# Gated delta rule steps with one combined product per chunk, and five modulation chunks summed later, in a two-block transformer kernel

## The reference, cut to what matters

```python
def step(S, inp):                       # one chunk of 64 tokens, per head
    qd, kc, val, att, kt, cd = inp
    v_new = val - kc @ S
    o = qd @ S + att @ v_new
    S = S * cd + kt.T @ v_new
    return S, o
# kc and val come from a 64x64 unit triangular solve per chunk and head
...
mod = silu(c) @ w_ada + b_ada           # 12 chunks of 512 columns
sh1, sc1, g1, sh2, sc2, g2 = split(mod, 6)
h = rmsnorm(x, norm_mix) * (1 + sc1) + sh1
proj = h @ w_in                         # 16 chunks of 512 columns
...
x = x + g1 * (merged @ w_out)
h2 = rmsnorm(x, norm_ffn) * (1 + sc2) + sh2
x = x + g2 * moe(h2)                    # 32 experts, top 2
```

## Time and profile before

| | |
|---|---|
| median of 3 runs | 1138.16 us (1137.22 to 1146.73) |
| profiled execution, its own time | 1137.32 us |
| its span | 1135.5 us, so 1.8 us lie around it |
| granted TensorE clock, mean | 0.998 |
| TensorE busy (PE) | 1106.6 us, 97% |
| TensorE weight loads (PEld) | 843.2 us, 74% |
| VectorE (DVE) | 603.9 us, 53% |
| ScalarE (ACT) | 501.5 us, 44% |
| GpSimd (POOL) | 151.2 us, 13% |
| delta steps | about 141.5 to 168 us of the span |
| feed-forward part begins | 192.6 us |
| product of step s = 3 ends | 427.1 us |

### The profile page before, as it was taken

The page is one execution under the profiler, slowest core; times in us unless marked ns, Lnnn a source line. Parts: engine busy times, 40 slices in busy tenths (PEclk is TensorE's granted clock), DMA queues, the critical chain, the costliest instruction groups (busy, mean ns, idle before and its releaser), DMA issues.

```text
span 1135.5 us, 18601 instructions
## 1 busy us (share of the span) xinstructions
PE 1106.6 (97%) x7625; PEld 843.2 (74%) x7625; DVE 603.9 (53%) x925; ACT 501.5 (44%) x827; POOL 151.2 (13%) x111
## 2 busy tenths in 40 slices
PE   8999799999999999999999999999999999999996
PEld 7987678999878888778888876666666666666663
DVE  5988676879956784785755652222222222222223
ACT  6665654654433746645556252222222222222223
POOL 1339960422000040400000000000000000000000
PEclk9999999999999999999999999999999999999999
DMA  9862825477486756644548579999999999999994
GB/s 314 280 215 77 297 93 201 161 263 257 183 306 204 243 176 223 211 162 154 174 157 329 209 288 423 421 426 423 423 425 420 425 422 421 425 424 421 426 421 175
DMA packets 82701, 332.05 MB, mean 292 GB/s; under 512 B 4555, under 2 KB 6926, under 8 KB 66110
## 3 DMA queue, kind: packets, MB, share of 16 engines
q1 hardware_dynamic: 81236, 328.43, 74.6%
q0 software_dynamic: 1088, 2.34, 1.0%
q10 hardware_dynamic: 298, 0.11, 0.1%
HBM read 329.83 MB, written 1.05 MB: 291 GB/s over the span
## 4 chain that ended last, share of the span: by engine, by line
PE 80%; DVE 8%; DMA 7%; issue 2%; ACT 2%; SPq 1%; DVEq 0%; ACTq 0%
PE bank L1113 18%; PE bank L451 12%; PE bank L453 12%; PE bank L452 12%; PE bank L1132 9%; PE bank L1103 5%; DMA ring<-in_w_exp_down 3%; DVE ring_r L1844 2%; DMA ring<-in_w_in 2%; DVE arena L1924 2%; PE bank L1160 1%; PE bank L1161 1%; DMA ring<-in_w_ff 1%; DMA ring<-in_w_ada 1%; PE bank L1120 1%
## 5 line engine op out<-in xcount | busy, mean ns | idle before, releaser
L1844 DVE TENSOR_TENSOR ring_r<-ring,arena_r 128x2048 fp32r<-128x2048 f32 x93 | 217.9, 2355 | 118.5 <-ACT arena_r L1333 116.9
L1333 ACT ACTIVATE arena_r<-ring 128x2048 fp32r<-128x2048 f32 x93 | 177.4, 1918 | 170.1 <-PE bank L453 71.7
L453 PE MATMUL bank<-arena_r,actT_r 128*128 128x512 f32 x384 | 150.5, 392 | 0.0
L451 PE MATMUL bank<-arena_r,tok_r 128*128 128x512 f32 x352 | 140.8, 400 | 1.7 <-DVE con L2331 1.7
L452 PE MATMUL bank<-ring_r,tok_r 128*128 128x512 f32 x352 | 138.2, 393 | 0.0
L2688 POOL TENSOR_TENSOR ring<-ring 128x512 f32<-128x512 f32 x63 | 102.5, 1652 | 253.7 <-ACT ring L1424 251.9
L2503 DVE TENSOR_TENSOR arena<-bank,arena 64x512 f32<-64x512 f32 x62 | 42.7, 688 | 175.3 <-PE bank L1132 174.6
L451 PE MATMUL bank<-tok_r,arena_r 128*128 128x256 f32 x352 | 99.5, 283 | 1.8 <-DVE actT_r L1861 1.2
L453 PE MATMUL bank<-tok_r,ring_r 128*128 128x256 f32 x352 | 98.3, 279 | 0.0
L452 PE MATMUL bank<-actT_r,arena_r 128*128 128x256 f32 x352 | 98.2, 279 | 0.0
L2489 DVE TENSOR_TENSOR arena<-bank,arena 128x256 f32<-128x256 f32 x32 | 13.6, 425 | 151.3 <-ACT arena L1763 93.9
(11 more groups left out here) (424 smaller groups left out, 1770.7 us busy)
## 6 DMA issues: line engine op xcount, KB each, us to landing
ring<-in_w_in SPq DMA_DIRECT2D x22, 2048.0 KB, 9.6
ring<-in_w_exp_down SPq DMA_DIRECT2D x22, 2048.0 KB, 21.3
ring<-in_w_exp_gate SPq DMA_DIRECT2D x21, 2048.0 KB, 21.9
arena<-in_w_exp_up SPq DMA_DIRECT2D x21, 2048.0 KB, 23.5
ring<-in_w_ff SPq DMA_DIRECT2D x16, 2048.0 KB, 7.8
ring<-in_w_ada SPq DMA_DIRECT2D x12, 2048.0 KB, 10.9
arena<-in_w_exp_gate SPq DMA_DIRECT2D x11, 2048.0 KB, 21.5
arena<-in_w_exp_down SPq DMA_DIRECT2D x10, 2048.0 KB, 21.4
```

The lines of the kernel that those rows point to most:

```text
L451: mm(o, l[0], r[0], start=start, stop=False)
L453: return mm(o, l[1], r[0], start=False, stop=stop)
L1333: A(hi, w, ACT.Copy).then_inc(S["w_high"], 1)
L1844: TT(half(i, ringR)[0], w, hi.bitcast(fp32), ALU.subtract).then_inc(S["w_rest"], 1)
```

## The change

It does four things.
1. `kc` and `qd` of a chunk stand side by side in `KQ`, so that one product of 128 rows gives both the correction and the output's state part. The masked products of two chunks are made together, behind step 1 and step 3, in two different quadrants of the array, into the banks of the combined products. The two `kc` banks of a t are filled in turns.
2. VectorE multiplies the old state by its decay before the product for the new state is there, and adds afterwards (two instructions in place of four). VectorE's other work in the steps is put in another order: `o_squares(0)`, `att_out(0)` and `w_rest(F0)` come later, and the second attention product is split into two parts.
3. Modulation chunks 0 to 4 leave the mixing stage. Chunk 0 is now summed by VectorE before `add_x`, 1 and 2 take the places of 5 and 6, 3 that of 7, and 7 and 8 move back by one place or more; 6, 4 and 5 are summed by VectorE in `steps2`, s = 3, 9 and 13. GpSimd does not sum anything in the mixing stage any more.
4. The order of the loads follows.

```diff
-        ET, DI, DT, YY, AT, MT = [x[:, 0:8 * C] for x in (ar(15360, 1024), DQ, DK, QD, kbT, qT)]
-        VAL, KC, VN = KB, QD, ar(15360, 1024)
+        ET, DI, DT, RR, AT, MT = [x[:, 0:8 * C] for x in (ar(15360, 1024), DQ, DK, QD, kbT, qT)]
+        YY = DQ[:, 8 * C:16 * C]
+        VAL, VN = KB, ar(15360, 1024)
+        KQ = [QD, qdT]
...
-        ADA_BY_POOL = (0, 4)
-        ADA_BY_DVE = (7, 8, 9)
-        DVE_MOD = {4: 8, 10: 9}
-        ADA_FF1 = {2: 5, 5: 6}
-        ADA_FF2 = {1: 7, 3: 8, 6: 9}
-        ADA_STEP = {3: 10, 6: 11}
+        ADA_BY_POOL = (1, 2, 10, 11)
+        ADA_BY_DVE = (0, 3, 7, 8, 9, 6, 4, 5)
+        DVE_FF2 = {3: 7, 5: 8, 10: 9}
+        DVE_STEP = {3: 6, 9: 4, 13: 5}
+        ADA_FF1 = {2: 1, 5: 2}
+        ADA_FF2 = {1: 3, 3: 7, 4: 8, 6: 9}
+        ADA_STEP = {3: 10, 4: 6, 6: 11, 10: 4, 14: 5}
...
-        ADA_BEHIND = {("win", 2): (0,), ("win", 6): (1, 2, 3, 4), ("ff1", 2): (5,), ("ff1", 5): (6,), ("ff2", 0): (7,),
-                      ("ff2", 3): (8,), ("ff2", 6): (9,), ("win2", 2): (10,), ("win2", 6): (11,)}
+        ADA_BEHIND = {("wout", 1): (0,), ("ff1", 2): (1,), ("ff1", 5): (2,), ("ff2", 0): (3,), ("ff2", 3): (7,),
+                      ("ff2", 4): (8,), ("ff2", 6): (9,), ("win2", 2): (10,), ("win2", 4): (6,), ("win2", 6): (11,),
+                      ("win2", 9): (4,), ("win2", 13): (5,)}
...
-                elif l == 1:
-                    ada(0)
                 elif l == 2:
-                    ada(1)
                     att_turn()
...
                     bk = begin(f"vp{n}")
                     for h in range(DH):
-                        o = (4 * t + h) * P
-                        i = mm(bk[r:r + C, h * P:(h + 1) * P], KC[:, o + r:o + r + C], old[:, h * P:(h + 1) * P],
-                               start=True, stop=True)
+                        i = mm(bk[:, h * P:(h + 1) * P], KQ[t][:, 256 * h + 2 * r:256 * h + 2 * r + P],
+                               old[:, h * P:(h + 1) * P], start=(h == 0), stop=True, skip_group_check=True)
                     end(i, f"vp{n}")
                     if n == 1:
                         prob_turn(range(4, 8))
+                    elif n == 2:
+                        end(att_values(begin("ao0"), 0, range(8)), "ao0")
                     else:
-                        att_values(n - 2)
-                        if n == 3:
-                            o_turn(0)
-                pe.wait_ge(S["vn_new"], n + 1)
+                        end(att_values(ao1, 1, range(4, 8)), "ao1")
+                    wait_read(pe, f"vp{n}")
...
-                bk = begin(f"do{n}")
-                for h in range(DH):
-                    ...
-                    if n:
-                        mm(bk[r:r + C, h * P:(h + 1) * P], qdT[:, o + r:o + r + C], old[:, h * P:(h + 1) * P],
-                           start=True, stop=False)
-                    i = mm(bk[r:r + C, h * P:(h + 1) * P], MT[...], VN[...], start=(n == 0), stop=True)
-                end(i, f"do{n}")
                 if n == 0:
                     prob_turn(range(4))
-            ada(4)
+                elif n == 2:
+                    ao1 = begin("ao1")
+                    att_values(ao1, 1, range(4))
+                else:
+                    two = [(0, begin("do0") if n == 1 else begin_at(f"do{n - 1}", where[f"vp{n - 1}"][0])),
+                           (C, begin_at(f"do{n}", where[f"vp{n}"][0]))]
+                    for h in range(DH):
+                        for q, bk in two:
+                            i = mm(bk[C - q:P - q, h * P:(h + 1) * P], MT[q:q + C, ...], VN[q:q + C, ...], ...)
+                            if h == DH - 1:
+                                end(i, f"do{n - 1 + q // C}")
+                    if n == 3:
+                        o_turn(0)
...
             out_product(1, 1, lambda: turn_x1(0))
+            ada(0)
...
@@ VectorE, behind the levels
             new_values(0)
-            mod_cols(3)
             new_state(0)
-            dve.wait_ge(S["a_exp"], AH)
-            step(V.reciprocal(a_rd, a_sum))
             prob_copies((1, 3))
             new_values(1)
-            prob_copies((5, 7))
             new_state(1)
+            prob_copies((5, 7))
             wait_read(dve, "val1")
+            new_values(2)
+            new_state(2)
+            dve.wait_ge(S["a_exp"], AH)
+            step(V.reciprocal(a_rd, a_sum))
             o_squares(0)
-            new_values(2)
+            new_values(3)
             att_out(0)
-            new_state(2)
             w_rest(F0)
-            new_values(3)
             o_tokens(0)
+            att_out(1)
             w_rest(F0 + 1)
-            att_out(1)
+            o_squares(1)
             o_rest(0)
             w_rest(F0 + 2)
-            o_squares(1)
             o_tokens(1)
             w_rest(F0 + 3)
             o_rest(1)
-            mod_cols(4)
...
+            mod_sums(0)
...
@@ ScalarE
-            ada_scaled(1)
...
-            ada_scaled(2)
...
-            ada_scaled(3)
```

More of the change, by code:

```diff
@@ L440, in ada @@
                 else:
-                    by_pool = [x for x in range(c + 1) if x not in ADA_BY_DVE]
-                    pe.wait_ge(S["pool_step"], 1 + 3 * len(by_pool) + sum(x <= c for x in ADA_BY_POOL))
+                    pe.wait_ge(S["pool_step"], 4 + 3 * ADA_BY_POOL.index(c))
                 w = weights("ada", c)
@@ L569, in _ @@
                 bk = begin(f"R{t}")
-                end(mm(bk[:, 0:256], K("blk"), YY[:, t * 256:(t + 1) * 256], start=True, stop=True), f"R{t}")
+                end(mm(bk[:, 0:256], K("blk"), RR[:, t * 256:(t + 1) * 256], start=True, stop=True), f"R{t}")
             split_product("win", 1, "ak")
@@ L1438, in _ @@
                     done(copy(dst[:, t * 512:(t + 1) * 512], bk[:, :]), f"dT{x}{t}")
+            wait_full(act, "dT31")
+            for t in range(T):
+                bk = wait_full(act, f"dT3{t}")
+                done(copy(v3(KQ[t], DH)[:, :, C:C + P], v3(bk[:, :], DH)), f"dT3{t}")
             w_high(12)
@@ L2053, in _ @@
                     biased_scores(range(4, 8))
-                    mod_cols(2)
                 masked(l, 1)
@@ L2075, in new_values @@
                     bk = wait_full(dve, f"vp{n}")
-                    TT(VN[rows, o], VAL[rows, o], bk[rows, :], ALU.subtract).then_inc(S["vn_new"], 1)
-                    dve.wait_ge(S["vn_new"], n + 1)
-                    dve.sem_inc(read[where[f"vp{n}"][0]], 1)
+                    done(TT(VN[rows, o], VAL[rows, o], bk[rows, :], ALU.subtract), f"vp{n}")
             def new_state(n):
-                t = n // 2
-                bk = wait_full(dve, f"sn{n}")
                 old, new = states[(n - 1) % 2], states[n % 2]
                 if n == 0:
-                    step(V.tensor_copy(new, bk[:, :]))
-                else:
-                    if n == 2:
-                        wait_full(dve, "do1")
-                    for h in range(DH):
-                        hs = slice(h * P, (h + 1) * P)
-                        step(STT(new[:, hs], old[:, hs], ecd[:, 8 * (n % 2) + 4 * t + h:8 * (n % 2) + 4 * t + h + 1],
-                                 bk[:, hs], ALU.mult, ALU.add))
-                dve.sem_inc(S["s_new"], 1)
-                dve.sem_inc(read[where[f"sn{n}"][0]], 1)
+                    bk = wait_full(dve, "sn0")
+                    done(V.tensor_copy(new, bk[:, :]), "sn0")
+                else:
+                    o = 8 * (n % 2) + 4 * (n // 2)
+                    wait_read(dve, f"sn{n - 1}")
+                    tt(v3(new, DH), v3(old, DH), bc(ecd[:, o:o + DH], P), ALU.mult)
+                    bk = wait_full(dve, f"sn{n}")
+                    done(TT(new, new, bk[:, :], ALU.add), f"sn{n}")
             def att_out(t):
@@ L2157, in _, with mod_sums @@
             o_rest(1)
-            mod_cols(4)
-            for c in range(4):
-                wait_read(dve, f"mod{c}")
-            step(STT(sc1, modc[:, 8:16], 1.0, col("nmix", 0, 8), ALU.add, ALU.mult))
+            def mod_sums(c):
+                n = place[("ada", c)]
+                dve.wait_ge(w_in[n % NR], 16 * (n // NR + 1))
+                w = weights("ada", c)
+                step(TS(w[:, 0, :], w[:, 0, :], cs[:, 0:1], None, ALU.mult))
+                for k in range(1, KT):
+                    i = STT(w[:, 0, :], w[:, k, :], cs[:, k:k + 1], w[:, 0, :], ALU.mult, ALU.add)
+                    if k < KT - 1:
+                        step(i)
+                i.then_inc(S["mod_summed"], 1)
+            mod_sums(0)
             def add_x(n, c, t):
@@ L2186, in _ @@
             n2_rest((2, 3))
+            mod_cols(0)
             for i in range(F1 + 1, F1 + NH):
@@ L2214, in _ @@
             TS(angle, angle, 3.1415925, -3.1415925, ALU.min, ALU.max).then_inc(S["ang_ready"], 1)
-            def mod_sums(c):
-                n = place[("ada", c)]
-                dve.wait_ge(w_in[n % NR], 16 * (n // NR + 1))
-                w = weights("ada", c)
```

(26 more changed lines are left out.)

73 lines of the change are left out of this document (33 added, 40 removed).

## The result

The changed kernel takes 1156.52 us (median of 4 runs, 1156.24 to 1157.51), the kernel before 1138.37 us beside it. The ratio is 1.015, with a 95% interval of 1.011 to 1.019: 1.5% slower.

A forecast was written before the change was run, and what follows sets the result against it. TensorE, busy 97% of the span, was taken as the bound, with the experts' loads setting the pace from about 680 us. -5.4 + 0.3 + 1.5 + 1.8 + 12.4 + 3.4 = +14.0 on 1137.3 gives 1151.3, stated as 1151.5; range 1140 to 1158.

The forecast's parts named there:

- Levels and steps, output product: Levels to output product: last values at 149.5 us, 11.4 won there; output product at 160.4 instead of 167.55.
- Where that gain goes: VectorE: Behind the steps: VectorE has 10.9 us of work before the output product, so of 11.4 us won 7.4 stay.
- Transposes of x: Before the feed-forward part: `mod_sums(0)`, 5.9 us on VectorE ahead of `add_x`, makes them 1.6 us late.
- Clock: Granted clock falls to half behind the pauses of 5.2 and 12.4 us, 1.7 us each: +3.4, bounds 0 and 6.
- Second feed-forward product: Loads ff2_5 and ff2_7 come late there, 1.2 and 1.0 us, residual sums 0.2: together +1.8, between -0.6 and +3.
- Load win2_5: `steps2`, s = 3: released only behind `ada(10)`, so TensorE's line 918 stands for 12.4 us; bounds 10.6 and 14.
- Sums in `steps2`: Sums of chunks 6, 4 and 5 on VectorE: only a wait of 0.2 us by `ada(4)` was charged.
- Rival (D): `steps2`: one of the sums of chunks 6, 4 and 5, 5.9 us each, is exposed as well: 1157; chance 0.05.
- The sum: Whole kernel: all terms give +14.0 us on 1137.3, so 1151.3, stated as 1151.5.
- Rival (B): `steps2`, s = 3: win2_5's load is hidden, so the kernel is not slower: 1137; chance 0.11.
- Two rules against the rows: Skill's rules on tiling-mode drains and load time (6.8 us, sum 1147) set aside for trace rows: no price, 11 us.

The follow-up runs named there:

- the moved-chunks half: Only point 3 (the moved modulation chunks), with the delta steps of the kernel before: 1155.4 us, 1.010 of the kernel before.
- the delta part: Only points 1 and 2 of the change, modulation chunks at the places of the kernel before: 1144.1 us, 1.001 of the kernel before.
- two delta-part kernels: Points 1 and 2 on the old chunk schedule, without and with a new VectorE and ScalarE order behind the steps: 1144.1 and 1133.6 us.
- the delta part with the list order: Points 1 and 2 on the old chunk schedule, plus VectorE's and ScalarE's new order around the steps' end: 1133.6 us, 0.991 of the kernel before.

## Why the prediction was right, point by point

- **Levels and steps, output product.** The time at which the last values come was foretold to 0.1 us (149.5, measured 149.6), and that of the output product too (160.4, measured 160.3). The two pauses on the way were 2.6 and 4.1 us, foretold as 2.4 and 5.2. "Where that gain goes: VectorE" holds, and was understated: the moved-chunks half reaches 160.7 without any of the new products, so 0.4 of the 7.5 us won there is the delta part's, and the half clock behind the pauses takes more than that back.
- **Transposes of x.** 1.6 us foretold, 1.5 measured.
- **Clock.** 1.7 us had been charged behind each long pause; 1.8 was measured both times. The row that the price came from does not carry it: in the windows of the kernel before from 1.2 to 6 us, with its 12 slow matmuls, the granted clock reads 1.00. The rows of the changed kernel do: line 922 took 3.71 us at 0.50, line 918 before 1.89 at full clock. So the size came out, but its source did not show it. The clock fell already behind the pause of 2.6 us (0.52 from 154.2 to 156.2), and behind that of 3.5 us too; neither had been charged.
- **Second feed-forward product.** The term of +1.8 us was mis-sized, and its upper bound of +3 with it. From the transposes of x to those of n3 the kernel lost 5.0 us, 2.5 more than foretold. I had followed each load to its own product, and missed the chain over a bank: late load, VectorE's split, `mod_cols(7)`, the bank for `ada(8)`, 3.5 us and a few matmuls at half clock.
- **Load win2_5.** The mechanism was the one foretold: the load issued behind `ada(10)`, ScalarE's copies behind its split, line 922 waiting for them. 12.4 us foretold, 10.4 measured, because the load was there 9.0 us after its issue and not after 11. The lower bound was put at 10.6; its own terms give 10.5.
- **Sums in `steps2`.** Rival (D), given 0.05, came on top of the forecast: 3.2 us before chunk 4, where I had counted 0.2. The row that I had set for it, the 1.7 us wait near s = 8, was the right warning.
- **The sum.** -2.0 for the pause, +2.5 for the feed-forward product, +3.0 for chunk 4 and +1.2 in the experts, not traced further, bring 1151.3 to 1156. The pause and the feed-forward term both lay outside the bounds that the prediction gave them, and the last two had none. That the time still fell into the range is in part luck: one error was of the other sign, and the range was 18 us wide.
- **Rival (B)** was wrong in its price. With that load hidden it gave 1137; two kernels hid the pause and took 1155. The pause was not a term that stands alone, but the first of several that lay behind each other.
- **Two rules against the rows.** The prediction read `do1` as 32 instructions in 2.9 us and found no price for alternating between places of 128 and of 64 rows. The trace of the kernel before has 16:

```profile
149.16 0.43 PE L749 MATMUL bank<-arena 128*64 128x128 f32 x2
149.52 0.43 PE L751 MATMUL bank<-arena 64*64 64x128 f32 x2
149.88 0.43 PE L749 MATMUL bank<-arena 128*64 128x128 f32 x2
...
149.52 0.19 PEld L751 LDWEIGHTS bank<-arena 64*64 64x64 f32 x2 [0.17 <-issue]
149.88 0.19 PEld L749 LDWEIGHTS bank<-arena 128*64 128x64 f32 x2 [0.17 <-issue]
```

  That is 0.36 us for two, 0.18 each, where line 728 or 751 alone takes 0.13, so a change costs 0.1 us, and the weight loads stand idle for 0.17 at each. The Trainium skill, TensorEngine Tiling (Array Packing), section Key Properties, has the array drain when the mode changes; the trace agrees, and the prediction was wrong to set the row against it. The sum does not move by it: the 2.9 us charged for each removed `do` came from this row and hold the price, an estimate of 0.8 us in each (16 times 0.05). In the changed kernel the pair, 16 instructions in two places of one size, takes 1.0 us. By the Trainium skill, DMA: Bandwidth & Descriptors, section Anatomy of one DMA, the load would have taken an estimated 6.8 us; the page fits that to loads that GpSimd issues, and SyncE issues these. 9.0 were measured, between it and the 11 of the row that I took.

## What to carry to other kernels

A pause that ends by one engine's late step can hide others that together are as long; before it is priced as a gain to be had, ask what each other engine and queue would be late with if it were gone, and test the mending alone. In a ring of few slots, count for every load the step in which its slot comes free and the step in which its first reader wants it, the reader that runs ahead and not TensorE. Work moved to an engine with idle time costs nothing only where that engine reaches it before the consumer does: here the same sums one place earlier in VectorE's list made 12.8 us, and a lighter chain on TensorE made nothing until VectorE's list behind it was put in order.

## What the runs showed of the hardware

Behind the same pause of 2.8 us in the last level, the granted clock stayed at 1.00 in the profile of the kernel before and went to 0.50 for 140 to 150 us in those of two delta-part kernels. The same kernel does either: of nine executions of the delta part with the list order, six took 1132 to 1134 us with a mean clock of 0.994 or more, three 1139 to 1141 with 0.989 or less. With the pause cut to 1.0 us all eight had a mean clock of 0.995 or more, though a pause of 2.0 us stands just ahead of it, at 130.2. The kernel before does the same: of its 73 executions beside the experiments, 35 took 1137 to 1139 us and 38 took 1145 to 1153. Where its clock falls in the slower ones no profile shows. What decides it between executions stays open.

In one 64x64 place 8 matmuls took 1.0 us from start to start, and 16 that take turns between two such places took 1.0 us too; matmuls that change between a 128-row and a 64-row place every two took 0.18 us each instead of 0.13.
